# RWKV-7 pipeline of a hybrid trunk: vector products, exponentials and group-norm spreading placed elsewhere in the stage

## The reference

```python
def step(s, inp):
    r_t, w_t, k_t, v_t, kk_t, a_t = inp
    sa = jnp.einsum("bhij,bhj->bhi", s, kk_t)
    s = (s * w_t[:, :, None, :] - sa[..., None] * (kk_t * a_t)[:, :, None, :]
         + v_t[..., None] * k_t[:, :, None, :])
    return s, jnp.einsum("bhij,bhj->bhi", s, r_t)
...
y = ys[0] + ys[1]
mu = jnp.mean(y, axis=-1, keepdims=True)
var = jnp.mean(jnp.square(y - mu), axis=-1, keepdims=True)
yn = ((y - mu) * lax.rsqrt(var + GN_EPS)).reshape(bn, t, B_WIDTH) * W["b_gn_w"][j] + W["b_gn_b"][j]
yn = yn + (bonus[0] + bonus[1]).reshape(bn, t, B_WIDTH)
g = jax.nn.sigmoid(gd) @ W["b_g2"][j]
return (yn * g).astype(pb.dtype), jnp.stack(finals, axis=1)
```

## Time and profile before

| | us |
|---|---|
| runs, median of 3 | 3417.05 (3403.87, 3417.05, 3417.43) |
| profiled execution, its own time | 3403.86 |
| its span | 3402.1 |
| RWKV stages and tail, tr of stage 0 to the last `yo` | 403.6 |
| stage lengths, tr to tr, stages 0 to 6 | 40.4, 45.9, 44.2, 51.1, 45.4, 54.1, 43.3 |
| from tr of stage 7 to the last `yo` | 79.1 |

### The profile page before, as it was taken

How to read it: one execution, slowest core, us unless ns; L and a number is a source line. 1 busy time by engine, 2 the same in 40 slices (tenths; PEclk the granted TensorE clock), 3 DMA queues, 4 the chain that set the end, 5 groups by cost and what they waited for, 6 DMA issues and landing times.

```text
span 3402.1 us, 65430 instructions
## 1 busy us (share of the span) xinstructions
PE 3087.7 (91%) x28476; PEld 2915.4 (86%) x28476; DVE 1610.6 (47%) x2436; ACT 965.3 (28%) x1628; POOL 0.2 (0%) x4
## 2 busy tenths in 40 slices
PE   7799999996678887899999999999998887999998
PEld 7799999995566665899999999999996547999998
DVE  2455555644345554546464645465314553432324
ACT  1222212323334342321212322212324553322222
POOL 0000000000000000000000000000000000000000
PEclk6799999996669887999999999999998777999999
DMA  6244444210000000244344344444212111222221
GB/s 208 78 130 118 123 125 118 69 34 0 15 5 6 6 5 11 73 132 135 107 136 117 91 114 130 113 130 125 73 55 53 17 32 50 72 71 80 68 81 56
DMA packets 393617, 268.89 MB, mean 79 GB/s; under 512 B 12203, under 2 KB 372934, under 8 KB 393286
## 3 DMA queue, kind: packets, MB, share of 16 engines
q1 hardware_dynamic: 393414, 265.90, 27.9%
HBM read 257.61 MB, written 4.06 MB: 77 GB/s over the span
## 4 chain that ended last, share of the span: by engine, by line
PE 86%; DVE 7%; ACT 3%; issue 2%; DMA 1%; SPq 0%; ACTq 0%; DVEq 0%
PE banks L2399 64%; PE banks L1628 2%; PE banks L2423 2%; PE banks L2354 2%; PE banks L1668 2%; PE banks L843 1%; PE banks L435 1%; PE banks L410 1%; PE banks L837 1%; PE banks L826 1%; PE banks L2430 1%; PE banks L898 1%; PE banks L420 1%; PE banks L725 1%; DVE h_lo_as_f L1418 1%
## 5 line engine op out<-in xcount | busy, mean ns | idle before, releaser
L2399 PE MATMUL banks<-h_hi,w_hi 128*128 128x320 f32 x3600 | 823.2, 310 | 20.3 <-DVE w_lo L2101 19.8
L2399 PE MATMUL banks<-h_lo,w_hi 128*128 128x320 f32 x3600 | 822.3, 310 | 0.0
L2399 PE MATMUL banks<-h_hi,w_lo 128*128 128x320 f32 x3600 | 821.4, 310 | 0.0
L2399 PEld LDWEIGHTS banks<-h_hi,w_hi 128*128 128x128 f32 x3600 | 603.0, 188 | 21.7 <-issue 20.9
L2399 PEld LDWEIGHTS banks<-h_hi,w_lo 128*128 128x128 f32 x3600 | 603.8, 188 | 0.0
L2399 PEld LDWEIGHTS banks<-h_lo,w_hi 128*128 128x128 f32 x3600 | 603.7, 188 | 0.0
L2399 PE MATMUL banks<-big_as_f32r,w_hi 128*128 128x320 f32 x2816 | 528.7, 309 | 5.4 <-DVE w_lo L2101 4.6
L2101 DVE TENSOR_TENSOR w_lo<-raw,w_hi 128x1024 fp32r<-128x1024 f32 x333 | 399.0, 1218 | 223.4 <-ACT w_hi L1985 222.7
L1985 ACT ACTIVATE w_hi<-raw 128x1024 fp32r<-128x1024 f32 x333 | 341.5, 1050 | 446.9 <-DMA raw<-ffn_w 297.8
L2399 PEld LDWEIGHTS banks<-big_as_f32r,w_hi 128*128 128x128 f32 x2816 | 441.5, 188 | 6.5 <-DVE w_lo L2101 5.4
L2246 DVE TENSOR_TENSOR work<-work,banks 128x640 f32<-128x640 f32 x88 | 72.2, 821 | 604.8 <-PE banks L2399 590.5
(11 more groups left out here) (349 smaller groups left out, 2819.9 us busy)
## 6 DMA issues: line engine op xcount, KB each, us to landing
raw<-ffn_w SPq DMA_DIRECT2D x272, 512.0 KB, 5.1
work<-mod_w SPq DMA_DIRECT2D x136, 512.0 KB, 3.8
raw<-w_in_c SPq DMA_DIRECT2D x24, 512.0 KB, 3.7
raw<-w_in_ab SPq DMA_DIRECT2D x21, 512.0 KB, 3.9
w_hi_as_f<-mod_w SPq DMA_DIRECT2D x8, 512.0 KB, 5.2
raw<-w_out_ab SPq DMA_DIRECT2D x8, 512.0 KB, 4.8
work<-big SPq DMA_DIRECT2D x64, 64.0 KB, 2.3
raw<-w_out_c SPq DMA_DIRECT2D x8, 512.0 KB, 4.9
```

The lines of the kernel that those rows point to most:

```text
L2399: ins = nc.tensor.matmul(ps[:, c, 0:HALF], w, v[:, k, c * HALF:(c + 1) * HALF], start=(k == 0 and w is hi and v is xh), stop=(k == kts - 1 ...
```

## The change

Four orders of calls are different; no operation is added or dropped from the computation, and the operands are the same.

- **Factor products.** `rh`, `al`, `kap` of the next stage stood behind level 5. Now `rh`, `al`, a new step `ka` (the first part of the former `kap`) and `kap` are spread over levels 3 to 5: one place later in odd turns than in even ones. `arr` and `beta` stay behind level 5.
- **Exponentials.** The three `exps` stood behind levels 2, 3 and 4 on ACT; now all stand behind level 2, ahead of `kk_root`. `cum` goes from between the two halves of level 1 to the place behind `t0`, ahead of the back end's `g`; `ht`, `q` and `m` each go up by half a level.
- **kk.** `mx` and `rc` go from level 2's end to level 3's end.
- **Group norm.** `var_spread` goes from the end of odd turns to the start of the next even one (turns 4, 6 and 8), behind xp, with 6 of the 10 units of `chunk_rows` between its two parts; `yg`, `yb`, `yo` go from the end of an odd turn into the next even one: ahead of `t0p`, and behind `z1`.

```diff
 def pe_rwkv(pe):
+                late = d == 0 and it > 1
+                if late:
+                    var_spread(it - 2, 0)
+                    pe.wait_ge(AB.s, AB.value("xp", s - 1))
+                    chunk_rows(s, range(6))
+                    var_spread(it - 2, 1)
                 if front:
                     pe.wait_ge(DP.s, DP.value("beta", s))
...
                 if back:
                     pe.wait_ge(AB.s, AB.value("xp", s - 1))
-                    chunk_rows(range(8))
+                    chunk_rows(s, range(6 if late else 0, 8))
...
                     if d and it:
                         variance(it - 1)
-                        var_spread(it - 1, 0)
-                        var_spread(it - 1, 1)
 def act_rwkv(act):
...
                     level(s, 2)
+                    if nxt:
+                        for part in range(3):
+                            exps(s + 1, part)
                     if d and it + 1 < BT:
                         kk_root(it + 1)
-                    if nxt:
-                        exps(s + 1, 0)
                     level(s, 3)
-                    if nxt:
-                        exps(s + 1, 1)
...
                     level(s, 4)
-                    if nxt:
-                        exps(s + 1, 2)
 def dve_rwkv(dve):
...
+                if d == 0 and it > 1:
+                    post(it - 2, "yg")
+                    post(it - 2, "yb")
                 dve.wait_ge(PF.s, PF.value("A", s))
...
+                if nxt:
+                    prep(s + 1, "cum")
                 if back:
                     for step in ("g", "ft", "z0", "rhop"):
                         back_end(s - 1, step)
                 level_p(s, 1)
                 if nxt:
-                    prep(s + 1, "cum")
+                    prep(s + 1, "ht")
+                    prep(s + 1, "q")
                 level_t(s, 1)
...
+                if d == 0 and nxt:
+                    prep(s + 1, "rh")
                 level_p(s, 4)
...
+                if nxt:
+                    prep(s + 1, "rh" if d else "al")
                 level_t(s, 4)
...
+                if nxt:
+                    prep(s + 1, "al" if d else "ka")
                 level_p(s, 5)
...
+                if nxt:
+                    prep(s + 1, "ka" if d else "kap")
                 level_t(s, 5)
                 if nxt:
-                    for step in ("al", "rh", "kap", "arr", "beta"):
-                        prep(s + 1, step)
+                    if d:
+                        prep(s + 1, "kap")
+                    prep(s + 1, "arr")
+                    prep(s + 1, "beta")
                 if d and it:
-                    for step in ("rc", "yn0", "yn1", "yg", "yb", "yo"):
+                    for step in ("rc", "yn0", "yn1"):
                         post(it - 1, step)
```

More of the change, by code:

```diff
@@ L641, in build @@
         DL = Steps(sem("wd_level"), [f"{k}{lev}" for lev in LEVS for k in "pt"])
-        DP = Steps(sem("wd_prep"), ["cum", "ht", "q", "m", "kd1", "kd", "al", "rh", "kap", "arr", "beta"])
+        DP = Steps(sem("wd_prep"), ["cum", "ht", "q", "m", "kd1", "kd", "rh", "al", "ka", "kap", "arr", "beta"])
         DK = Steps(sem("wd_k"), ["mul", "mx", "rc", "n0", "n1"])
@@ L844, in level_x, with chunk_rows @@
                 ins.then_inc(PL.sem(f"X{lev}"), 1)
+            def chunk_rows(s, us):
+                for u in us:
+                    for p in range(2):
+                        b = (6, 7, 0)[u // 4]
+                        ins = mm(bank(b)[heads[p], u % 4 * P:u % 4 * P + P], w_tt[heads[p], u * L:(u + 1) * L],
+                                 w_av[(s - 1) % 2][heads[p], u, :], start=True, stop=True)
+                return ins
             pe.wait_ge(b_load, 48)
@@ L929, in pe_rwkv @@
                 if back:
-                    chunk_rows(range(8, 10)).then_inc(PB.sem("wu"), 1)
+                    chunk_rows(s, range(8, 10)).then_inc(PB.sem("wu"), 1)
                 if nxt:
@@ L1109, in exps @@
                     af(w_d1[s % 4], w_ht, ACT.Exp, scale=-DECAY).then_inc(AP.sem("ex"), 1)
+                else:
+                    ins.then_inc(AP.sem(f"e{part}"), 1)
             def v_rows(it, part):
@@ L1278, in prep @@
                     v.tensor_tensor(kd, kd, big[:, it + T_K, :], ALU.mult).then_inc(q, 1)
+                elif step == "rh":
+                    dve.wait_ge(AP.s, AP.value("e1", s))
+                    v.tensor_tensor(rh, rh, b3(big[:, it + T_R, :]), ALU.mult).then_inc(q, 1)
                 elif step == "al":
@@ L1433, in dve_rwkv @@
             kk(0, "n1")
-            for step in ("kd1", "kd", "al", "rh", "kap", "arr", "beta"):
+            for step in ("kd1", "kd", "rh", "al", "ka", "kap", "arr", "beta"):
                 prep(0, step)
@@ L1440, in dve_rwkv @@
                 if not front:
+                    for step in ("yg", "yb", "yo"):
+                        post(BT - 2, step)
                     bonus(BT - 1, "bn")
@@ L1491, in dve_rwkv @@
                     back_end(s - 1, "z1")
+                if d == 0 and it > 1:
+                    post(it - 2, "yo")
                 level_t(s, 2)
@@ L1494, in dve_rwkv @@
                     back_end(s - 1, "z2")
-                if d and it + 1 < BT:
-                    kk(it + 1, "mx")
-                    kk(it + 1, "rc")
                 if d == 0 and it:
@@ L1507, in dve_rwkv @@
                     back_end(s - 1, "z4")
+                if d and it + 1 < BT:
+                    kk(it + 1, "mx")
+                    kk(it + 1, "rc")
                 if nxt:
```

22 lines of the change are left out of this document (9 added, 13 removed).

## The result

The changed kernel took 3367.11 us (median of 4 runs, 3366.30 to 3369.19) against 3416.57 of the kernel before; the ratio is 0.987 (95% interval 0.9847 to 0.9894). A second set gave 3361.16 us (3355.43 to 3366.43) and 0.9859 (0.9819 to 0.9898). In some fifty runs more the kernel before had medians of 3408 to 3410, so the change is worth 41 to 49 us. All of these runs but one lie between 3395 and 3427 us; that one took 5029 us at a granted clock of 0.548 and enters no ratio. The forecast was 3380 in a range of 3358 to 3403, and a gain of 32.

A forecast was written before the change was run, and what follows sets the result against it. The prediction took a chain of waits between engines, none of them full, to bound the stages and tail. Terms of 24.1 us by order and 8 by clock gave 32 off the kernel: 3380 us, range 3358 to 3403.

The forecast's parts named there:

- Even into odd, and into 2: Turns into stages 1, 3, 5, 7 and 2: moved products let tr start earlier, gaining 13.3 and 2.2 us.
- Into 4 and 6: Turns into stages 4 and 6: overlapped spreading shortens the chain to tr from 9.8 to 6.4 us; 4.8 in all by order.
- Tail: After the last stage: spreading and `chunk_rows` finish earlier by 5.9 us, 3.3 of it by order.
- Level 3 of odd stages: Stages 1, 3, 5: with `mx` behind level 3, that level is 1.3 us shorter each, 3.9 in all.
- Products inside the levels: Levels 3 to 5: the moved products mostly hide in DVE's waits and cost 3.4 us in all.
- swallowing rival: Levels 3 to 5: DVE bounds them, so moved products eat much of the gain, leaving 12 us, 3405; chance 0.14.
- Front of even stages, and `cum`: Stage starts: `yg`, `yb` delay `t0p` in 4 and 6, costing 1.2 us; moving `cum` out of level 1 gains 1.2.
- Order in all: The stages and tail: all reordering terms together, without any change of clock, gain 24.1 us.
- Clock: tr, xp and the tail: closing PE's waits brings the fast rate; 8 us taken, between 0 and 12.3.
- the clock gives nothing: At the turns: order gains as worked out but tr stays at 3.4 us; gain 20 to 28, chance 0.17.
- likeliest case: The whole kernel: order and part of the clock together gain 28 to 42 us; chance 0.55.
- More: Inside the levels: the clock stays up there also, for a gain of 42 to 55 us, 3365; chance 0.09.

The follow-up runs named there:

- a0_again: The changed kernel run again with no edit; 3361.16 us, ratio 0.9859 to the kernel before.
- a7_yg_later_fill: The changed kernel with two idle matmuls behind each `level_q`, and `yg`, `yb`, `yo` moved behind `m`, `z1`, `z3`; 3344.13 us.
- b3_fill_all: The kernel before with idle matmuls behind each `level_q`, ahead of tr of odd stages and stage 2, and ahead of the spreading; 3369.86 us.
- b1_fill: The kernel before with idle matmuls only where PE waits at the turns, no order changed; 3393.59 us, ratio 0.9964.
- a1_products_back: The changed kernel with its factor products behind level 5 again, all else as changed; 3396.86 us, ratio 0.9969.
- a6_products_back_fill: The changed kernel with factor products behind level 5 again, idle matmuls behind each `level_q` and ahead of tr of odd stages and stage 2; 3363.67 us.
- a3_root_first: The changed kernel with `kk_root` ahead of the exponentials again and `mx`, `rc` at level 2's end; 3376.90 us, ratio 0.9896.
- b0_again: The kernel before run again with no edit; its profiled run took 3416.56 us, ten runs have a median of 3408.81.

## Why the prediction was right, and where it was not

- **What bounds.** Right: with no engine full, only chains counted. Span outside the part moved by 1.2 us.
- **Even into odd, and into 2.** The forecast was 3.7 us less into 3, 5 and 7, 2.3 into 1 and 2.2 into 2. Measured from the subtraction's end to tr, 5.67, 5.67 and 5.72 became 2.00, 2.01 and 2.05; 4.79 became 2.39, and 4.00 became 1.80. Right to a tenth.
- **Into 4 and 6.** Forecast 9.8 to 6.4. Measured 9.84 to 5.55, except 9.15 into 6 in the first profile, where the slow rate stretched it. 0.9 better, since the spreading takes 1.09 at the fast rate; I had priced it at the slow one, 1.98, from every row that I had looked at. With the clock up in both orders it is 7.69 to 5.96, so 3.5 for the two by order, where the sum has 4.8.
- **Tail.** Forecast 3.3 by order. With the clock up in both orders 39.0 against 36.0 remain behind the levels, 3.0.
- **Level 3 of odd stages.** This is a step that failed in its mechanism. It said that with `mx` behind level 3 "the level is about 1.3 shorter" and that `kk_spread` would be wanted "at 1213.7 instead of 1215.0". Level 3 came to 5.14 in two of the three stages of a0_again and in most of the runs with idle matmuls (5.83 to 6.26 in the first profile), but level 4 took back all of it: 3.9 of the sum were worth 0. Without idle matmuls it was a loss, if anything: levels 3 and 4 of stages 1, 3 and 5 took 38.7 and 39.9 us together in the two profiles before, and 43.2 and 41.0 in the two after, with level 4 at 8.0 to 8.7 instead of 6.4 to 7.3, mostly at the slow rate. The forecast of what is late next stopped at ACT's copy and did not go on to PE, which stands ahead of the spreading until root, maximum and reciprocal are through.
- **Products inside the levels.** Forecast -3.4, measured about -2.0 (0.35 in stage 1, 0.53 in 3 and 5, 0.2 in 2, 4, 6). The swallowing rival is out.
- **Front of even stages, and `cum`.** Forecast -1.2 and +1.2. a7_yg_later_fill shows that `yg` and `yb` do cost 0.64 in the front of stage 4. Level 1 of stages 0 to 6, from which `cum` went, is 3.60 at its shortest instead of 3.93.
- **Order in all.** Forecast 24.1, measured 23.9 by the parts and 22.0 by the medians. That the first agrees so well is luck: level 3's 3.9 were too much, the turns came out 0.4 under the forecast, and what makes up for that are, among others, products that cost 1.4 less, a shorter level 1, and a late level in b3_fill_all.
- **Clock.** The mechanism was right, the size was not: 8 forecast, and 12.3 as the most. All of the gain less the order's is 41 to 49 less 22 to 24, 17 to 27 us. I took two thirds of what I had counted in tr, xp and the tail, and the levels as they were. b1_fill shows that the waits at the turns alone are worth 12 in the kernel before, and a1_products_back against a6_products_back_fill (30 to 36 us without fill, 16 to 19 with it) that the products' waits cost as much again by the clock as by the chain. In the change, the fronts are 11.1 us shorter in the first profile, 9.0 of it tr. The rival "the clock gives nothing" is out: tr took 1.83 in five stages. By the rule that the Trainium skill (TensorE: Matmul & The Clock Gate, Part 4: PE-mode transpose) gives for transposes, that the full clock doesn't engage for them, tr would have stayed at 3.4; this case's traces disagree with it.
- **The base.** 3380 was worked out from a median of 3417 that lay 8 or 9 us above that of the many runs since; from 3408 the forecast gain gives 3376. The rest of the miss is the clock. Against the 3416.57 measured beside it, the gain is 49.5 us. That is above the 28 to 42 of the likeliest case and in the range of the rival *More*, whose reason did not hold: in the profile the clock did not stay up in the levels, which had 7 slow groups instead of 8 and took 205.9 us instead of 202.9.

Still open: the 16 us of a3_root_first. With fill the same edit costs 2.4 us, inside the scatter, so nearly all of them are slow stretches; why that order has more of them, two of the three in stages that it doesn't touch, no run tells. That the idle time of PE as such, and not the length of single waits, sets the levels' rate wasn't separated either.

The version that beats both is the changed kernel with two idle matmuls behind each `level_q`: 3347.83 us, 60 below before and 13 below the change. Whether a7_yg_later_fill (3344.13) is better still, the runs don't tell.

## What to carry to other kernels

When no engine is full, trace one turn of the pipeline from what released the first instruction, and move what stands in that chain into waits that the same engine has elsewhere; such a sum can be right to a few tenths of a microsecond for each turn, as it was here for the turns into odd stages. Follow a moved wait two engines on, since the one that is late next may hold the same chain. Where TensorE stands still for microseconds, price the matmuls behind the wait at both rates, and try idle matmuls in the waits: they separate order from clock, and can be a gain in themselves (12 and 13 us here).

## What the runs showed of the hardware

- The same matmuls take 1.8 times as long behind a stretch in which TensorE stood still: 15 transposes 3.43 against 1.83 to 1.89 us, the spreading 1.98 against 1.09, five level transposes 1.33 against 0.77. With idle matmuls at the turns and in the levels (b3_fill_all) tr of stages 1 to 7 takes 1.83 to 1.86 and xp 1.38 in each of these turns, and 3 of the 40 groups of level transposes are still slow; with those at the turns alone (b1_fill) two xp stayed at 2.40. The windows of tr of stage 3 and of what follows it, before, show the level:

```profile
1084.06:1087.50 3.44, 3.44 (x19) 3.11 (x23) 0.00 (x0) 0.00 (x0) 0.00 (x0) 0.50 0.02 5
1087.50:1090.00 2.50, 2.50 (x64) 2.50 (x68) 1.22 (x1) 2.08 (x6) 0.00 (x0) 1.00 0.00 0
```

  0.50 is 1.2 GHz, directly behind 4.24 us of standing still; from 1087.50 to 1090.00, with PE busy throughout, it was 1.00, 2.4 GHz.
- Two executions of one kernel differ by 9.0 us in a part of 400: 8 and 11 slow groups at a granted clock of 0.85 and 0.81 before, 7 and 4 at 0.89 and 0.91 after. The runs of one kernel spread over some 30 of 3400 us, and not all of that lies in this part: behind it, b0_again was 5.0 longer than the first profile of the same kernel.
- Two 128x128 f32 matmuls (four rows) behind each `level_q` cost next to nothing where PE waits anyway: levels 3 and 4 of an even stage take 4.84 and 5.14 us with and without them at the fast rate. In the turns into 4 and 6, where PE is waited for, they cost 0.4 each.
